# Expert loop of a one-core decoder layer: ten turns of three sure and two conditional rounds in place of thirty turns of one and one

## What is computed

```python
def hier_moe(xn, w_rg, b_rg, w_re, b_re, w_gate, w_up, w_down):
    ...
    expert = gsel[:, None] * EXPERTS_PER_GROUP + top_i      # two of 32 experts for each token
    ...
    def expert_block(args):
        xb, e = args
        h = jax.nn.silu(xb @ w_gate[e]) * (xb @ w_up[e])
        return h @ w_down[e]
    ybuf = lax.map(expert_block, (buf.reshape(nb, MOE_BLOCK, d), block_e)).reshape(nb * MOE_BLOCK, d)
    y = ybuf[dest].astype(F32) * sw[:, None]
    return jax.ops.segment_sum(y, st, num_segments=T).astype(xn.dtype)
```

## Time and profile before

| what | value |
|---|---|
| median of 3 runs | 2376.75 us (2374.35 to 2377.93) |
| the profiled execution's own time | 2374.06 us |
| its span in the trace | 2371.9 us |
| PE busy over the span | 2160.0 us (91%) |
| DVE, ACT, POOL busy | 1403.9, 973.1, 459.1 us |
| mean granted clock of TensorE | 0.964 of full speed |

### The profile page before, as it was taken

How to read it: one execution, slowest core, us unless ns; L and a number is a source line. 1 busy time by engine, 2 the same in 40 slices (tenths; PEclk the granted TensorE clock), 3 DMA queues, 4 the chain that set the end, 5 groups by cost and what they waited for, 6 DMA issues and landing times. The chain is left out here.

```text
span 2371.9 us, 41848 instructions
## 1 busy us (share of the span) xinstructions
PE 2160.0 (91%) x14293; PEld 1248.0 (53%) x14294; DVE 1403.9 (59%) x2100; ACT 973.1 (41%) x1458; POOL 459.1 (19%) x342
## 2 busy tenths in 40 slices
PE   6999999999979898999999999649999999999990
PEld 3565564565658783455555555325555555555550
DVE  7556566555559874333333333398667777777763
ACT  5432532432331343222222222217566676767653
POOL 0022121121130000000000000023434343434433
PEclk9999999999989999999999999769999999999995
DMA  8101001002041134112112110349889999999957
GB/s 249 50 27 63 1 27 63 1 27 47 1 169 62 63 125 170 41 49 71 45 63 72 36 45 36 113 151 324 294 256 326 310 342 347 350 332 335 341 177 299
DMA packets 159471, 349.62 MB, mean 147 GB/s; under 512 B 28782, under 2 KB 39406, under 8 KB 159104
## 3 DMA queue, kind: packets, MB, share of 16 engines
q1 hardware_dynamic: 140128, 310.32, 36.1%
q0 software_dynamic: 18080, 33.59, 6.2%
q10 hardware_dynamic: 1152, 4.19, 0.5%
HBM read 299.81 MB, written 57.15 MB: 150 GB/s over the span
## 5 line engine op out<-in xcount | busy, mean ns | idle before, releaser
L2665 PE MATMUL bankE<-wgu,xT 128*64 128x512 f16 x3840 | 430.6, 381 | 23.3 <-issue 11.6
L2665 PEld LDWEIGHTS bankE<-wgu,xT 128*64 128x64 f16 x3840 | 219.4, 110 | 226.0 <-issue 40.5
L2546 DVE SCALAR_TENSOR_TENSOR wgu<-w_rows,wgu 128x2048 f16<-128x2048 f32 x128 | 284.8, 2285 | 36.7 <-ACT wgu L2314 36.7
L111 PE MATMUL bankA<-main_room,hnT 128*128 128x512 f16 (+1 forms) x1536 | 301.8, 354 | 2.8 <-DVE main_room L639 2.8
L2257 POOL DMA_INDIRECT scratch_ybuf<-y,rows x80 | 175.1, 2188 | 375.6 <-DMA scratch_ybuf<-y,rows 269.2
L2314 ACT ACTIVATE wgu<-w_rows 128x2048 f16<-128x2048 f32 x128 | 234.3, 1899 | 30.8 <-issue 26.8
L111 PEld LDWEIGHTS bankA<-main_room,hnT 128*128 128x128 f16 x1536 | 150.7, 98 | 145.5 <-issue 8.7
L2665 PE MATMUL bankE<-wd,hT 128*64 128x512 f16 x1920 | 222.5, 381 | 0.5 <-ACT hT L2345 0.5
L111 PE MATMUL bankA<-hnT,main_room 128*128 128x512 f16 x768 | 173.6, 389 | 9.0 <-issue 6.8
L2546 DVE SCALAR_TENSOR_TENSOR wd<-w_rows,wd 128x2048 f16<-128x2048 f32 x64 | 143.8, 2288 | 54.8 <-ACT wd L2314 51.8
L111 PE MATMUL bankC<-w_out_s,catT 128*128 128x512 f16 x768 | 170.1, 382 | 2.5 <-DVE w_probs L1917 2.5
(11 more groups left out here) (385 smaller groups left out, 2980.7 us busy)
## 6 DMA issues: line engine op xcount, KB each, us to landing
w_rows<-in_w_gate SPq DMA_DIRECT2D x64, 1024.0 KB, 7.1
w_rows<-in_w_up SPq DMA_DIRECT2D x64, 1024.0 KB, 8.2
w_rows<-in_w_down SPq DMA_DIRECT2D x64, 1024.0 KB, 8.8
cat_t<-scratch_cat SPq DMA_DIRECT2D x16, 512.0 KB, 4.9
main_room<-in_x SPq DMA_DIRECT2D x16, 512.0 KB, 5.5
scratch_ybuf<-main_room SPq DMA_DIRECT2D x16, 512.0 KB, 2.6
out<-hf SPq DMA_DIRECT2D x16, 512.0 KB, 10.9
x_room<-in_x SPq DMA_DIRECT2D x3, 2048.0 KB, 10.8
```

Source lines behind the costliest of these rows:

```text
L111: ins = pe.matmul(o, a[x][k], b[y][k], start=start and k == 0 and j == 0, stop=stop and k == n - 1 and j == 2)
L2546: dve.scalar_tensor_tensor(place(p, slot, 1), room(p), W_SCALE, place(p, slot, 0), ALU.mult, ALU.subtract).then_inc(done, 1)
L2665: ins = pe.matmul(o(half), tokens(x, k), rows(z, k, half), start=k == 0 and j == 0, stop=k == n - 1 and j == 2, skip_group_check=True)
```

## The change

A turn of the loop becomes five rounds: three that always run and two that run only if the turn's number is below a count. Turns go from 30 to 10. The smallest number of rounds stays 30. The table of first rounds in `plan` gets 10 entries in place of 30, and is built in two steps that add, to three times the turn's number, the extra rounds of the turns ahead. Each round's steps are the same as before.

```diff
-ROUNDS = MIN_TURNS
+LOOPS, SURE, MORE = 10, 3, 2
+assert MIN_TURNS == LOOPS * SURE and MAX_TURNS <= LOOPS * (SURE + MORE)
...
-            with eng.Fori(0, ROUNDS) as t:
-                n = eng.value_load(plan[0:1, bass.ds(PL_FIRST + t, 1)], min_val=0, max_val=MAX_TURNS - 1)
-                for p in range(2):
-                    step(n * 2 + (4 + p), p)
-                with eng.If(t + ROUNDS < used):
+            with eng.Fori(0, LOOPS) as t:
+                n = eng.value_load(plan[0:1, bass.ds(PL_FIRST + t, 1)], min_val=0, max_val=MAX_TURNS - SURE - 1)
+                for i in range(SURE):
                     for p in range(2):
-                        step(n * 2 + (6 + p), p)
+                        step(n * 2 + (4 + 2 * i + p), p)
+                for i in range(MORE):
+                    with eng.If(t + (MIN_TURNS + i * LOOPS) < used):
+                        for p in range(2):
+                            step(n * 2 + (4 + 2 * (SURE + i) + p), p)
...
-            do(ts, first_f[:, :], turns_f[:, :], -float(ROUNDS), None, ALU.add)
-            do(stt, plan[:, PL_FIRST:PL_FIRST + ROUNDS], iota[0:1, 0:ROUNDS], first_f[0:1, :], iota[0:1, 0:ROUNDS], ALU.min, ALU.add)
+            turn, at_turn = iota[0:1, 0:LOOPS], t32[0:1, 0:LOOPS]
+            do(ts, at_turn, turn, float(SURE), None, ALU.mult)
+            for i in range(MORE):
+                do(ts, first_f[:, :], turns_f[:, :], -float(MIN_TURNS + i * LOOPS), 0.0, ALU.add, ALU.max)
+                do(stt, plan[:, PL_FIRST:PL_FIRST + LOOPS] if i == MORE - 1 else at_turn, turn, first_f[0:1, :], at_turn, ALU.min, ALU.add)
```

More of the change, by code:

```diff
@@ L2087 @@
 MAX_TURNS = NB // 2 - 2
-ROUNDS = MIN_TURNS
+LOOPS, SURE, MORE = 10, 3, 2
+assert MIN_TURNS == LOOPS * SURE and MAX_TURNS <= LOOPS * (SURE + MORE)
 NBT = NB + 2
-PL_BLOCK, PL_SPLIT, PL_EXPERT, PL_TURNS, PL_MORE, PL_FIRST, PL_END = np.cumsum([0, NBT, NBT, NE, 1, 1, ROUNDS]).tolist()
+PL_BLOCK, PL_SPLIT, PL_EXPERT, PL_TURNS, PL_MORE, PL_FIRST, PL_END = np.cumsum([0, NBT, NBT, NE, 1, 1, LOOPS]).tolist()
 X_SCALE, H_SCALE, G_SCALE = 2.0 ** 2, 2.0 ** -3, 2.0 ** 14
```

## The result

The changed kernel takes **2525.85 us** (median) beside 2376.93 of the kernel before on the same chip: ratio 1.0624, 95% interval 1.0599 to 1.0649. Each median is of six runs, of which one took over 5000 us and isn't counted in the ratio; without it the medians are 2523.88 and 2376.75 us. The direction was forecast, the size was not: 147 to 149 us in place of 71, outside the range (2380 to 2498).

What follows compares the result with a forecast made beforehand. PE was taken to bound the loop, with DMA close behind. From 2374.06 us, -14.8 (joints) + 0.7 (plan) + 68.3 (code waits) + 17 (clock) gave 2445 us, range 2380 to 2498.

Steps and rivals of the forecast that it cites:

- What bounds the loop, and how often things happen: Expert loop: PE bounds it, DMA close behind; 38 rounds in 10 turns, 8 of four rounds and 2 of three.
- Term 1: Joints between loop turns: 29 become 9, those left at 0.87 us plus 0.37 per second skipped check; gain 14.8 us.
- Term 2: Plan built ahead of the loop: three more small DVE instructions, all of which count, 0.7 us more.
- Term 3: PE's loop code: a body of 12.5 blocks doesn't stay, so 21 jumps wait 3.25 us each, 68.3 us more.
- Term 4: PE's clock behind joints: standing over 7 us lowers it, 1.7 us lost each of ten times, 17 us more.
- In sequence nothing is lost: PE's code inside a turn: blocks fetched in sequence cost nothing, steps still come at 8.70 us.
- Other engines at nothing: ACT's and DVE's longer loop bodies cost nothing, covered by slack and PE's lateness; without that cover at least 10 x 2.0 us.
- (a): Rival on PE's loop code: all that a turn uses stays, terms 3 and 4 vanish, 2360 us; chance 0.14.
- (c): Rival: all as forecast, and ACT's and DVE's code waits show too, 3 us in ten turns, 2475 us; chance 0.09.

Runs made afterwards that it cites:

- the run with PE alone: Changed kernel with only PE running the new loop of ten turns, ACT and DVE keeping the thirty turns of before: 2526.92 us (one run).
- the run in which ACT stood up to 9.4 us: Kernel before with only ACT and DVE given the new loop of ten turns, PE keeping thirty: 2423.70 us, ratio 1.0192.

## Why the prediction was wrong

- **What bounds the loop, and how often things happen**: right. Ten turns, 21 waits at the places named, 207 packets on q8 (nearly 200 forecast), 8.70 us a step elsewhere.
- **Term 1, joints**: forecast -14.8. Beside their waits the nine joints cost 9.3, which would make -14.1, but that it comes so near is luck: 4.4 of it is late blocks of code in the last steps of three turns. The joints themselves cost 4.9, 0.5 each, where 0.87 and more was put down.
- **Term 2, the plan**: right. 0.7 forecast; the end of the chain, from the same instruction to the same instruction, takes 0.6 longer. PE came to the loop 3.1 us later, but 1.4 of that is there ahead of the chain's changed end (1567.77 against 1566.41) and the rest behind it, where nothing was changed.
- **Term 3, the code**: here the prediction failed. The mechanism was right, the price of a wait was not: 3.25 us forecast, 131.3 / 21 = 6.25 measured, so 131.3 in place of 68.3. These 63 us are most of the 76 that the two profiled executions lie further apart than was forecast. The price was taken from a small load on a quieter queue, with the DMA engines at 0.94 in this stretch, and for one block. That is about what one block then cost without other traffic (3.4, in the kernel with PE's code halved). In traffic it is some 6, and most jumps back wait while two blocks come, at 7.3. The upper bound of 4.7, a weight piece's landing less its own transfer, was no ceiling: at a DMA share of 0.43 a wait was still 4.9.
- **Term 4, the clock**: the mechanism was right, 1.7 us a joint forecast, 2.3 measured (20.4 behind the nine joints; 17 were forecast, with the loop's end as the tenth).
- **In sequence nothing is lost**: wrong, though small. Late blocks cost the 4.4 named above and some 3.4 in other steps.
- **Other engines at nothing**: right in the sum, as the run with PE alone is as slow as all three. What they cost without the cover was put at 20 or more; it is 48.
- **The rivals**: (a), code that stays, was wrong, yet its 2360 is what a body of 5.4 blocks then gave. (c) had the right effect on ACT and DVE, and no share in the time.

Of the two rules weighed, the first (the Trainium skill, Runtime: NRT & Kernel Launch, section Instruction fetch mechanics: a taken branch out of the window waits for a fetch) agrees with these runs in its mechanism, and not with its window of two blocks on PE: 5.4 blocks stay. The second (the Trainium skill, Advanced Engine Details and Errata, section ISA Cache: 128 KB for TensorE in lines of 16 KB) would let one think that 6.8 blocks stay, and they don't. It can be brought together with the runs if blocks that the body only cuts into, and those fetched ahead, take lines too; no run shows that.

## What to carry to other kernels

A loop's body has a size in instructions, and it counts every copy and every branch not taken: look at the queues of kind instruction, and unroll only as far as they stay silent. When they didn't here, every far jump cost PE some 6 us that nothing hid, and its clock besides. To make a joint cheap, take work out of it (a count in a register, no table, no check) before making joints fewer.

## What the hardware showed that was not expected

- PE keeps a loop body of 5.4 blocks of 256 instructions, and not one of 6.8. ACT's 499 and DVE's 548 instructions (counted in the programs) don't stay as a pair either; the 205 and 224 of the kernel before do.
- A jump of PE to code that is gone takes about 6.0 us when one block comes late and 7.3 to 7.5 when two do, while weights are loaded; with hardly any other transfer it takes 3.4 and 4.6 to 5.1. PE's branch record holds the wait. ACT's and DVE's branch records stay under 0.1 us in the run in which ACT stood up to 9.4 us.
- A loop whose count is in a register costs PE 0.03 us a turn here at most joints, where PE's queued matmuls cover it.
